# The last FFN of a hybrid encoder step works on 576 of its 592 token columns

## The reference

```python
for l in range(DEPTH):
    hp = hp + 0.5 * swiglu(rms_norm(hp, norm_ffn1[l]), ffn1_wg[l], ffn1_wu[l], ffn1_wd[l])
    hs = hs + 0.5 * swiglu(rms_norm(hs, norm_ffn1[l]), ffn1_wg[l], ffn1_wu[l], ffn1_wd[l])
    ...   # mixer: HGRN2 recurrence and selected attention (l = 0), causal pooling (l = 1)
    hp = hp + 0.5 * swiglu(rms_norm(hp, norm_ffn2[l]), ffn2_wg[l], ffn2_wu[l], ffn2_wd[l])
    hs = hs + 0.5 * swiglu(rms_norm(hs, norm_ffn2[l]), ffn2_wg[l], ffn2_wu[l], ffn2_wd[l])
y_prompt = hp[:, N_META:]
return (y_prompt, hs, ...)
```

## Time and profile before

| | |
|---|---|
| median of 3 runs | 2174.45 us (2172.32 to 2175.32) |
| the profiled execution's own time | 2178.14 us |
| its span, first to last instruction | 2176.4 us |
| mean granted TensorE clock | 0.957 of full speed |
| busy: TensorE, VectorE, ScalarE, GpSimd | 92%, 62%, 51%, 36% |
| last FFN, first gated matmul | 1788.25 us |
| last FFN, first down matmul | 2034.26 us |
| last write to `resid`, start | 2172.81 us |

### The profile page before, as it was taken

How to read it: one execution, slowest core, us unless ns; L and a number is a source line. 1 busy time by engine, 2 the same in 40 slices (tenths; PEclk the granted TensorE clock), 3 DMA queues, 4 the chain that set the end, 5 groups by cost and what they waited for, 6 DMA issues and landing times. The chain is left out here.

```text
span 2176.4 us, 35434 instructions
## 1 busy us (share of the span) xinstructions
PE 1996.0 (92%) x13900; PEld 1508.1 (69%) x13900; DVE 1358.7 (62%) x2050; ACT 1111.3 (51%) x1334; POOL 778.2 (36%) x446
## 2 busy tenths in 40 slices
PE   4999999999998788979999997999999678999999
PEld 2677777665776655657777775777777456777777
DVE  7777853314987743276787437778743667778632
ACT  5677854112143234057778335777843217778621
POOL 4766500000037402147571014776400426667000
PEclk9999999997998889989999999999999879999999
DMA  3223222210111020012222211332322201322221
GB/s 134 85 93 113 92 100 80 87 49 5 63 59 63 6 87 20 20 39 97 97 97 100 107 66 39 108 104 97 101 99 73 79 3 60 115 97 92 99 105 40
DMA packets 24025, 167.06 MB, mean 77 GB/s; under 512 B 3024, under 2 KB 3024, under 8 KB 8176
## 3 DMA queue, kind: packets, MB, share of 16 engines
q1 hardware_dynamic: 22176, 157.98, 20.9%
q0 software_dynamic: 1744, 7.66, 1.0%
HBM read 161.80 MB, written 3.83 MB: 76 GB/s over the span
## 5 line engine op out<-in xcount | busy, mean ns | idle before, releaser
L1661 PE MATMUL ps<-big 128*128 128x296 f16 x2464 | 717.2, 291 | 39.6 <-ACT big L667 12.4
L1665 PE MATMUL ps<-big 128*128 128x296 f16 x2464 | 716.6, 291 | 13.1 <-DVE big L1013 12.8
L1662 PE MATMUL ps<-big 128*128 128x296 f16 x2464 | 716.9, 291 | 0.0
L1642 PE MATMUL ps<-big 128*128 128x296 f16 x4224 | 540.0, 291 | 10.5 <-DVE big L1113 10.4
L1642 PEld LDWEIGHTS ps<-big 128*128 128x128 f16 x4224 | 411.2, 98 | 133.4 <-DVE big L1113 11.7
L384 POOL TENSOR_TENSOR big<-big 128x512 f32<-128x512 f32 x88 | 123.4, 1402 | 634.5 <-ACT big L558 388.0
L1661 PEld LDWEIGHTS ps<-big 128*128 128x128 f16 x2464 | 242.1, 98 | 119.1 <-issue 16.1
L1665 PEld LDWEIGHTS ps<-big 128*128 128x128 f16 x2464 | 242.2, 98 | 91.1 <-DVE big L1013 20.9
L1636 PE MATMUL ps<-big 128*128 128x296 f32 x992 | 264.6, 429 | 34.3 <-DVE big L1571 25.3
L1662 PEld LDWEIGHTS ps<-big 128*128 128x128 f16 x2464 | 242.4, 98 | 67.7
L1636 PEld LDWEIGHTS ps<-big 128*128 128x128 f32 x992 | 195.2, 198 | 98.8 <-issue 25.4
(11 more groups left out here) (270 smaller groups left out, 2074.2 us busy)
## 6 DMA issues: line engine op xcount, KB each, us to landing
big<-in_w_up SPq DMA_DIRECT2D x88, 1024.0 KB, 4.8
big<-in_w_dn SPq DMA_DIRECT2D x32, 1408.0 KB, 6.0
big<-in_w_in SPq DMA_DIRECT2D x20, 512.0 KB, 3.5
big<-in_w_out SPq DMA_DIRECT2D x1, 4096.0 KB, 12.7
resid<-in_x SPq DMA_DIRECT2D x4, 592.0 KB, 6.6
out_y<-resid SPq DMA_DIRECT2D x8, 296.0 KB, 4.7
big<-in_w_ai POOLq DMA_DIRECT2D x1, 2048.0 KB, 10.1
big<-in_w_pool POOLq DMA_DIRECT2D x1, 1024.0 KB, 5.2
```

Source lines behind the costliest of these rows:

```text
L1642: last = mm(ps[:, bank + hf, 0:HALF], w, x[:, hf * HALF:(hf + 1) * HALF], start=start, stop=stop)
L1661: mm(out, w[:, 0, c], xop[:, 0, x, c], start=start, stop=False, skip_group_check=True)
L1662: mm(out, w[:, 1, c], xop[:, 0, x, c], start=False, stop=False, skip_group_check=True)
L1665: last = mm(out, w[:, 0, c], xop[:, 1, x, c], start=False, stop=(c == DC // 2 - 1), skip_group_check=True)
```

## The change

In the last FFN alone (`f` = 3) every operation takes 288 columns in place of 296 for each half. The halves are columns 16 to 303 and 304 to 591; the 16 meta columns are left out, and their values in `resid` stay those from before the FFN (they are written out with y and dropped by the host). The number, order and waits of the instructions stay as they are, and so do all buffers' places; only the first 288 columns of each place are used. Operations that took one run of 592 or 1184 columns now take two or four runs of 288, through one more dimension in their address pattern.

```diff
+FFN_COLS = 3 * [HALF] + [(NT - N_META) // 2]
...
-        hjunk = work[:, 3 * NT:4 * NT].bitcast(F16)
+        hjunk = work[:, 3 * NT:4 * NT].bitcast(F16).rearrange("p (a n) -> p a n", a=4)
...
-                a.activation(ps[:, 3 * b + 1, 0:HALF], ps[:, 3 * b, 0:HALF], ACT.Copy).then_inc(p1_done[b], 1)
+                a.activation(ps[:, 3 * b + 1, 0:FFN_COLS[f]], ps[:, 3 * b, 0:FFN_COLS[f]], ACT.Copy).then_inc(p1_done[b], 1)
...   (the same cut in keep_p5, keep_u2, the three SiLUs, hidden_rows, x_highs, mix_x)
-                a.activation(hid16[:, c, 0], hid[:, c + 2], ACT.Copy, scale=hscale[:, part:part + 1]) \
+                a.activation(ffn_cols(f, hid16[:, c, 0]), ffn_cols(f, hid[:, c + 2]), ACT.Copy, scale=hscale[:, part:part + 1]) \
...
-                    cols = slice(h * HALF, (h + 1) * HALF)
-                    v.scalar_tensor_tensor(xf[:, c, cols], resid[:, c, cols], gains16[:, stage, c:c + 1],
-                                           rnorm_all[:, cols], ALU.mult, ALU.mult).then_inc(x_scaled, 1)
+                    first = NT - 2 * FFN_COLS[f] + h * FFN_COLS[f]
+                    cols = slice(first, first + FFN_COLS[f])
+                    v.scalar_tensor_tensor(xf[:, c, h * HALF:h * HALF + FFN_COLS[f]], resid[:, c, cols],
+                                           gains16[:, stage, c:c + 1], rnorm_all[:, cols], ALU.mult, ALU.mult) \
+                        .then_inc(x_scaled, 1)
...   (the same cut in low, mix, sum_c22, sum_c12, hidden_first, hidden_second, hidden_rest, hidden_low)
-                    r = split(resid[:, bass.ds(c, 1), :].rearrange("p a n -> p (a n)"))
-                    v.scalar_tensor_tensor(r, halves(4 * b), wback[:, b:b + 1], r, ALU.mult, ALU.add) \
+                    n = FFN_COLS[f]
+                    r = split(resid[:, bass.ds(c, 1), NT - 2 * n:NT].rearrange("p a n -> p (a n)"))
+                    v.scalar_tensor_tensor(r, halves(4 * b)[:, :, 0:n], wback[:, b:b + 1], r, ALU.mult, ALU.add) \
...
-                    last = mm(ps[:, bank + hf, 0:HALF], w, x[:, hf * HALF:(hf + 1) * HALF], start=start, stop=stop)
+                    last = mm(ps[:, bank + hf, 0:n], w, x[:, hf * HALF:hf * HALF + n], start=start, stop=stop)
...
-                out = ps[:, 3 * b + at, 0:HALF]
+                out = ps[:, 3 * b + at, 0:FFN_COLS[f]]
...
-                    mm(out, w[:, 0, c], xop[:, 0, x, c], start=start, stop=False, skip_group_check=True)
+                    mm(out, w[:, 0, c], xop[:, 0, x, c, 0:FFN_COLS[f]], start=start, stop=False, skip_group_check=True)
...
+def ffn_cols(f, ap):
+
+    return ap.rearrange("p (h n) -> p h n", h=2)[:, :, 0:FFN_COLS[f]]
```

More of the change, by code:

```diff
@@ L1020, in mix @@
                         dve.wait_ge(x_mixed, 6 * f + k + 1)
-                    left = xf[:, lo, HALF:NT] if t == 0 else xf[:, hi, HALF:NT]
-                    right = xf[:, lo, 0:HALF] if t == 0 else tf[:, 0, lo] if t == 1 else xf[:, lo, HALF:NT]
-                    v.tensor_tensor(tf[:, t, lo], left, right, ALU.subtract).then_inc(x_mixed, 1)
+                    own, other = slice(0, FFN_COLS[f]), slice(HALF, HALF + FFN_COLS[f])
+                    left = xf[:, lo, other] if t == 0 else xf[:, hi, other]
+                    right = xf[:, lo, own] if t == 0 else tf[:, 0, lo, own] if t == 1 else xf[:, lo, other]
+                    v.tensor_tensor(tf[:, t, lo, own], left, right, ALU.subtract).then_inc(x_mixed, 1)
                 for c in range(4):
@@ L1638, in product, with product_part, product16, product_step @@
                 return last
[L1640 removed]
+            def product_part(bank, w, x, n, start, stop):
                 for hf in range(2):
[L1642 removed]
+                    last = mm(ps[:, bank + hf, 0:n], w, x[:, hf * HALF:hf * HALF + n], start=start, stop=stop)
                 return last
[L1645 to L1652, removed]
+            def product16(bank, w_high, w_low, x_high, x_low, cols, k, n):
+                product_part(bank, w_high, x_high, cols, k == 0, False)
+                product_part(bank, w_high, x_low, cols, False, False)
+                return product_part(bank, w_low, x_high, cols, False, k == n - 1)
+            def product_step(f, b, name, signal, x_waits=None):
                 q, x, at = PRODUCTS[name]
                 w = w16[:, b, :, q * QW:(q + 1) * QW].rearrange("p a (c n) -> p a c n", c=DC // 2)
[L1656 removed]
+                out = ps[:, 3 * b + at, 0:FFN_COLS[f]]
                 for c in range(DC // 2):
@@ L1660, in product_step @@
                         pe.wait_ge(x_high, x_waits[0] + c // 2)
-                    mm(out, w[:, 0, c], xop[:, 0, x, c], start=start, stop=False, skip_group_check=True)
-                    mm(out, w[:, 1, c], xop[:, 0, x, c], start=False, stop=False, skip_group_check=True)
+                    mm(out, w[:, 0, c], xop[:, 0, x, c, 0:FFN_COLS[f]], start=start, stop=False, skip_group_check=True)
+                    mm(out, w[:, 1, c], xop[:, 0, x, c, 0:FFN_COLS[f]], start=False, stop=False, skip_group_check=True)
                     if x_waits and c % 2 == 0:
                         pe.wait_ge(x_waits[1], x_waits[2] + c // 2)
-                    last = mm(out, w[:, 0, c], xop[:, 1, x, c], start=False,
+                    last = mm(out, w[:, 0, c], xop[:, 1, x, c, 0:FFN_COLS[f]], start=False,
                               stop=(c == DC // 2 - 1), skip_group_check=True)
```

55 lines of the change are left out of this document (30 added, 25 removed).

## The result

The changed kernel takes 2164.3 us, median of 6 runs (2162.6 to 2167.2), against 2174.9 us of the kernel before (6 runs, 2171.9 to 2180.5): ratio 0.9946, 95% interval 0.9930 to 0.9962. The forecast was 2166.1 us in a range of 2162.9 to 2169.2.

A forecast was written before the change was run, and what follows sets the result against it. The last FFN was taken as bound by TensorE's matmul spacing, except at its start, the turn into the down part and perhaps late pairs; 0.57 + 5.12 - 0.75 + 0.32 + 3.08 + 0.02 = 8.36 off 2174.45 gave 2166.1 us (2162.9 to 2169.2).

The forecast's parts named there:

- Spacing: Last FFN: matmuls stand 0.1258 us apart at 296 columns, and each shrinks by 3.33 ns with eight columns less.
- Rival (c): Matmul spacing is held by the weight load: only 0.8 us gained, 2173.7 us; chance 0.06 with the skill page's variant (2171.8).
- Start to the second pair: Last FFN's start up to P4 of the second pair: shorter operations save 0.57 us, bounds 0.3 to 0.8.
- Given back in the pairs: VectorE's weight work, stretched by GpSimd, makes TensorE wait in middle and late pairs: -0.75 us, bounds -0.2 and -2.5.
- the 0.35 forecast: Middle pairs: some wait 0.13 us and some none, taken as 0.07 x 5 = 0.35 us lost.
- the 0.40 of the late pairs: Two late pairs where TensorE already waits: 0.20 us lost in each, since TensorE shrinks by 0.32 and VectorE and ScalarE by 0.12.
- Last pair to the second down unit: Chain over ScalarE and VectorE saves 0.32 us (0.2 to 0.4); TensorE's 2.6 us wait grows to 3.0.
- The clock: Behind the wait at the second down unit the clock falls, costing 1.62 us; kept as it is.
- rival (a): The clock stays up behind the second down unit's wait: 1.6 us more gained, 2164.5 us; chance 0.18.
- Down units: Down units two to eight: 924 matmuls at 3.33 ns each save 3.08 us.
- Rival (d): VectorE becomes the bound in every pair, beside GpSimd's additions: slower, 2201 us; decides from 0.8 us lost per pair; chance 0.02.
- Nothing may move before 1786 us: Sign expected in the changed profile: all stages ahead of the last FFN keep their times.

## Why the prediction was right, and where it was off

The forecast lies near the measured time, but partly by luck. The pairs gave back 0.7 us more than forecast, and the clock, kept up in two of three profiles of the changed kernel, gave 1.2 us on average that the forecast didn't have. Without the clock's part the last FFN gained 7.7 us, against 8.34 summed. What the measured 10.6 has beyond 8.9 is not the last FFN's, by the marks.

*Spacing.* 3.33 ns a matmul was right to the last digit, and the rule that float32 matmuls of three widths gave holds for fp16 at 256 to 296 columns. Rival (c) and the slope of the Trainium skill (TensorE: Matmul & The Clock Gate, section Back-to-back issue gap) fell with it: 132 matmuls would have gained 0.14 us by that slope and gained 0.44.

*Start to the second pair.* 0.57 expected, 0.63 measured, in all three profiles alike.

*Given back in the pairs.* The mechanism was right (VectorE's chain stretched by GpSimd, at P4, with a late pair's `seed_p1` beside it), the size was not. -0.75 fits the first profile, but over three profiles each 194.66 - 190.98 = 3.7 us are gained where TensorE alone gains 5.1: -1.4, between forecast and the bound of -2.5. Cut at P4 of the eighth pair, this divides as follows. The six middle pairs before it cost nothing over TensorE's own time before the change and 0.4 to 0.5 us after it: the 0.35 forecast was nearly right. From there to the last row total the loss was 1.1, 0.5 and 1.1 us before and is 1.3, 2.1 and 2.1 after, on average 0.96 more. So the term that was mis-sized is the 0.40 of the late pairs. It had both late pairs lose only TensorE's saving less that of the other engines. In the second and third profiles the waits for `seed_p1` themselves grew, from 0.6 us at most to 1.0 and 1.1. Ahead of that wait stand two L1193 (L1185 before), then the next unit's scale and ScalarE. In the second profile of the changed kernel:

```profile
1981.18 3.38 DVE L1193 SCALAR_TENSOR_TENSOR big<-big,scales 128x576 f16<-128x576 f32 x2
...
1986.98 0.30 PE L1669 MATMUL ps<-big 128*128 128x288 f16 x1 [1.04 <-ACT ps L604]
```

and in its first:

```profile
1982.05 2.56 DVE L1193 SCALAR_TENSOR_TENSOR big<-big,scales 128x576 f16<-128x576 f32 x2
```

The two took 3.38 and 3.40 us in the profiles with the wait of 1.0 or 1.1, 2.56 in the one with 0.2, and 1.94 with GpSimd on a quarter of the columns, where there is no wait. Before the change it was 3.09, 2.59 and 3.15, with 0.6, 0 and 0.6 us. So here too it is GpSimd's additions beside them that make the difference. Why they fall so in one execution and otherwise in the next isn't known.

In the middle pairs the reckoning by the overlap (0.14 us for 0.28 us more) had the cost wrong though the sum came out: the cost doesn't grow with the overlap. At that place L1115 takes 2.34 us, or 3.35 to 3.37 if GpSimd still works when it starts, and nothing between. Over the seven of them that start between 1860 and 2000 us in each of three profiles it was the long one 4 times in 21 before (1, 2 and 1) and 9 times in 21 after (4, 3 and 2). But a long one costs the pair little. In the changed kernel's middle pairs it began 4.8 to 5.4 us behind the pair's start and the short one 5.5 to 6.2, and `sum_c22` ended 8.5 to 9.1 us behind the pair's start with a long one and 8.2 to 8.9 with a short one, where P4 is due at 8.85. In the second and third profiles the late pairs that lost most had the short one.

*Last pair to the second down unit.* 0.32 expected, 0.33 measured, but the wait didn't grow to 3.0 us: it is 2.63. The stretch came out although this part of the reckoning was wrong. I had let the first down unit run at TensorE's pace. Its last ten chunks follow the ten L1185 at 0.82 us each, slower than their six matmuls (0.74), so TensorE's end hangs on VectorE there too, and both ends of the wait move together.

*The clock.* Kept as it was, and it did fall in the first profile. Of the eight profiles with TensorE on 288 columns in the last FFN, five kept it up there; of the three of before, none did; in the earlier FFNs, whose wait is the same 2.6 us in all kernels but the two that shorten it, both occur too. So rival (a), given 0.18, had more like an even chance (two of the changed kernel's own three profiles), and its 1.6 us are part of the measured gain in some runs. What decides it wasn't found.

*Down units.* 3.08 expected, 3.28 measured; 924 x 3.33 ns and 0.2 us from a clock that came back a little earlier.

*Rival (d)* needed 0.8 us lost in each pair. At 288 columns the pairs of the first profile, from P4 to P4, took 20.64 to 21.23 us, so 0.6 us at most over TensorE's own time; in the other two one late pair took 22.06, 1.4 us over, and the rest 21.26 or less. At 256 columns it is there, 1.5 us in nearly every pair, and still doesn't undo the gain.

*Nothing may move before 1786 us.* That was too strict a sign: three executions of the unchanged kernel reach the last FFN at 1785.5 to 1788.7 us, so a single pair of profiles can't be held to it.

## What to carry to other kernels

Where matmuls stand back to back, columns saved are worth their time at the clock, and other widths in the same trace give the price. But count which of them stand behind a wait whose other side doesn't shrink, and look how much slack the next engine has: here it was 0.2 us of 21 or somewhat more in the middle pairs and none in the late ones, so of the first eight columns' time three quarters were gained in the up part, and of the next sixteen's less than half. Before a few microseconds are put down to a change, cut two traces at the same marks: 3.3 of the first 11.9 us lay in code that wasn't touched, and a third profile of the old kernel was needed to see that it was chance.

## What was not expected of the hardware

The same program came back to the upper clock 3 us after a wait of 6.4 us in one execution and 6 us after it in another, worth 2.6 us of 2175. VectorE's 128 x 2048 operation takes 2.35 us alone and 3.36 with 1.2 us of a GpSimd addition over its start; yet a middle pair in which it does so is hardly longer, since the operation begins earlier there.
